# Mixer of a two-block transformer: projections in rounded parts, six buffers for high parts, one early expert place less

## The reference

```python
def split_cols(p): ...          # p = h @ w_in: q, f forward, f backward, v, gates
def gates(z, lb):               # f = lb + (1 - lb) * sigmoid(z); keys 1 - f, decays log(f)
def qv(p):                      # q = silu(p[2]) * 128 ** -0.5; v = p[5]
# each chunk: cum = cumsum(log f)
#   o = q * exp(cum) @ state + sum over earlier tokens of (q . k * exp(cum_t - cum_s)) v_s
#   state = exp(cum_end) * state + (k * exp(cum_end - cum)).T @ v
# out = rmsnorm(o) * silu(p[6]), merged with the attention under sigmoid(p[7]) and sigmoid(p[8])
```

## Time and profile before

| | us |
|---|---|
| median of 3 runs | 3784.51 |
| lowest, highest | 3781.16, 3787.37 |
| the profiled execution | 3779.92 |
| its span | 3778.1 |
| PE busy in the span | 3637.9 (96%) |
| DVE, ACT, POOL busy | 1917.7, 1146.6, 360.3 |

### The profile page before, as it was taken

One profiled execution on the slowest core, in us unless ns is written; L12 is line 12 of the kernel. 1 busy time (PEld: TensorE's weight loads), 2 busy tenths in 40 slices (PEclk: granted clock), 3 DMA queues, 4 the chain that ended last, 5 costly groups with the idle time before them and its releaser, 6 DMA issues.

```text
span 3778.1 us, 55586 instructions
## 1 busy us (share of the span) xinstructions
PE 3637.9 (96%) x23568; PEld 2589.5 (69%) x23568; DVE 1917.7 (51%) x3415; ACT 1146.6 (30%) x1733; POOL 360.3 (10%) x213
## 2 busy tenths in 40 slices
PE   8999999999999999999999999999899999999997
PEld 7799888888887998888987865767633333333333
DVE  4588576768664885767696333556421111111111
ACT  3243344444532433444445212333210000000011
POOL 0044300000000432000000000212000000000000
PEclk9899999999998999999999999999899999999999
DMA  5544344445446444444454312211489999999996
GB/s 200 211 174 163 135 168 177 160 177 181 169 153 227 164 163 139 158 178 178 175 172 171 133 66 100 90 67 64 163 371 421 427 428 427 427 428 427 428 427 271
DMA packets 81024, 846.24 MB, mean 224 GB/s; under 512 B 8896, under 2 KB 11072, under 8 KB 12512
## 3 DMA queue, kind: packets, MB, share of 16 engines
q1 hardware_dynamic: 80768, 842.60, 56.8%
HBM read 841.52 MB, written 1.05 MB: 223 GB/s over the span
## 4 chain that ended last, share of the span: by engine, by line
PE 83%; DMA 10%; DVE 4%; ACT 2%; issue 1%; POOL 0%; DVEq 0%; ACTq 0%; SPq 0%
PE bank L88 81%; DMA ring<-in_w_gu_dram 10%; ACT arena L114 1%; PE bank L101 1%; DVE arena L124 1%; DVE arena L138 1%; DVE arena L168 0%; DVE arena L156 0%; DVE arena L132 0%; DMA ring<-in_w_inA_dram 0%; ACT L114 0%; DVE arena L144 0%; DVE ring_rounded L124 0%; POOL ring_rounded L124 0%; DVE arena L130 0%
## 5 line engine op out<-in xcount | busy, mean ns | idle before, releaser
L88 PE MATMUL bank<-arena 128*128 128x32 f16 (+7 forms) x8020 | 922.2, 328 | 37.0 <-DVE arena L124 11.9
L88 PEld LDWEIGHTS bank<-arena 128*128 128x128 f16 (+4 forms) x8020 | 502.4, 132 | 451.3 <-issue 335.7
L124 DVE TENSOR_TENSOR arena<-arena 128x512 f16<-128x512 f16 (+6 forms) x768 | 531.9, 719 | 55.8 <-ACT arena L114 40.4
L114 ACT ACTIVATE arena<-bank 128x256 f32<-128x256 f32 (+2 forms) x443 | 203.0, 458 | 1164.3 <-PE bank L88 940.2
L88 PE MATMUL bank<-ring,arena 128*64 128x512 f32 (+1 forms) x1968 | 502.8, 596 | 39.7 <-DMA ring<-in_w_gu_dram 36.2
L88 PE MATMUL bank<-xhi,ring_rounded 128*128 128x256 f32 x1744 | 489.2, 280 | 0.0
L88 PE MATMUL bank<-xhi,uhi 128*128 128x256 f32 x1552 | 453.0, 292 | 6.5 <-DVE ring_rounded L124 5.8
L88 PE MATMUL bank<-xlo,uhi 128*128 128x256 f32 x1552 | 437.1, 282 | 0.0
L88 PEld LDWEIGHTS bank<-ring,arena 128*64 128x64 f32 (+1 forms) x1968 | 170.3, 144 | 361.2 <-issue 281.9
L88 PE MATMUL bank<-vhi,phi 128*128 128x512 f32 x1024 | 408.0, 398 | 2.0 <-DVE ring_rounded L124 2.0
L88 PE MATMUL bank<-vhi,plo 128*128 128x512 f32 x1024 | 403.5, 394 | 0.0
(11 more groups left out here) (144 smaller groups left out, 3216.9 us busy)
## 6 DMA issues: line engine op xcount, KB each, us to landing
ring<-in_w_gu_dram SPq DMA_DIRECT2D x97, 2048.0 KB, 23.8
ring<-in_peer_u_dram SPq DMA_DIRECT2D x128, 1024.0 KB, 6.7
ring<-in_peer_v_dram SPq DMA_DIRECT2D x128, 1024.0 KB, 5.1
arena<-in_w_dn_dram SPq DMA_DIRECT2D x62, 2048.0 KB, 22.4
arena<-in_w_gu_dram SPq DMA_DIRECT2D x43, 2048.0 KB, 22.3
ring<-in_w_hg_dram SPq DMA_DIRECT2D x14, 2048.0 KB, 8.4
ring<-in_w_mod_dram SPq DMA_DIRECT2D x12, 2048.0 KB, 7.8
ring<-in_w_inA_dram SPq DMA_DIRECT2D x8, 2048.0 KB, 7.8
```

Source lines behind the costliest of these rows:

```text
L88: i = self.e.matmul(o, l, r, start=start, stop=stop)
L114: self.e.activation(o, i, f, scale=scale, **kw).then_inc(self.sem, 1)
L124: self.e.tensor_tensor(o, a, b, op).then_inc(self.sem, 1)
```

## The change

Each projection of the state model becomes three rounded matmuls per slice. h is split into a high part (`uhi`, `xhi`) and a low part (`h_r`, on the place of h) after the gates of the attention are projected. Each task's weights, 1024 columns, are split into a high part, a copy to the rounded type on ACT (`act_high`), and a low part, weights minus high on POOL (`pool_low`), which takes the weights' own place. PE multiplies high by high, high by low, low by high. A v task becomes a quarter of the input slices for all tokens, and four v banks are copied out after the last.

The tasks are numbered 0 to 47 in PE's order (`in_turn`). There are six buffers for high parts, two in `xlo` and four in the ring place that the attention's last q weights leave; the ring is left with two places. `highs` sets how far the parts are made at each step: numbers 0 to 5 in the attention; 6 and 7 among the first f tasks; 8, 9 after the log, 10, 11 after the exp of the keys, 12, 13 before the kdT copies, 14 to 17 in the levels of unit 0. Unit 1: 18, 19 after the sigmoid, 20, 21 after the log, 22, 23 after the exp of the keys, 24, 25 before kdT, 26 to 29 in the levels. Unit 2: 30 to 32, 33 and 34, 35, 36 and 37, 38 to 41 likewise. Unit 3: 42, 43; 44, 45; none; 46, 47.

The tasks of unit 1's readout and of unit 2 change places: one q task in the readout, then three q and four v. The early expert piece is no longer fetched; the first two pieces come when all tasks are done ("hg parts").

```diff
+HIGHS = 6
@@
-        before_keys = {0: q_tasks(0) + v_tasks(0), 1: gate_tasks(0), 2: q_tasks(1) + v_tasks(1)[1:], 3: gate_tasks(1)[:6]}
+        before_keys = {0: q_tasks(0) + v_tasks(0), 1: gate_tasks(0), 2: q_tasks(1)[1:] + v_tasks(1), 3: gate_tasks(1)[:6]}
...
-        in_readout = {0: v_tasks(1)[0:1], 1: []}
+        in_readout = {0: q_tasks(1)[0:1], 1: []}
@@ pe_task
-            P.wait_ge(*at["landed", ("w_hg", kind, k)])
+            P.wait_ge(*at["hg split", kind, k, ct])
...
-                P.mm(b[:, 0:cols], [(w[:, dc, cs], hT[:, dc, 0:cols]) for dc in range(8)])
+                P.mm(b[:, 0:cols], [(w[:, dc, :], h) for dc in range(8) for w, h in
+                                    ((hi, h_high(dc)[:, 0:cols]), (hi, h_lo[:, dc, 0:cols]), (lo, h_high(dc)[:, 0:cols]))])
...
+        def act_high(i):
+            if i < len(in_turn):
+                kind, k, ct = in_turn[i]
+                A.wait_ge(*at["landed", ("w_hg", kind, k)])
+                if i >= HIGHS:
+                    A.wait_ge(*at["hg", *in_turn[i - HIGHS]])
+                A.act(task_high(kind, k, ct), task_of(kind, k, ct), ACT.Copy)
+                A.mark("hg high", kind, k, ct)
+        def pool_low(i):
...
+                G.wait_ge(*at["hg high", kind, k, ct])
+                G.tt(task_low(kind, k, ct), task_of(kind, k, ct), task_high(kind, k, ct).bitcast(F32), SUB, lag=FREE)
+                G.mark("hg split", kind, k, ct)
+        def highs(u, step, k=0):
+            a, n = number[before_keys[u][0]], len(before_keys[u])
+            till = {"first": min(a + 4, a + 3 + k), "sigmoid": a + 4, "log": a + 6, "keys": a + n, "before": a + n + 2,
+                    "level": a + n + (2, 3, 3, 4, 4, 5, 6)[k]}[step]
+            since = made[0]
+            made[0] = max(since, min(till, len(in_turn)))
+            return range(since, made[0])
@@ pool_mixer
+                for step in ("sigmoid", "log", "keys"):
+                    pool_lows(u, step)
...
+                pool_level(u, 0)
+                pool_level(u, 1)
+                pool_lows(u, "before")
                 for lv in range(7):
-                    pool_level(u, lv)
+                    if lv < 5:
+                        pool_level(u, lv + 2)
+                    pool_lows(u, "level", lv)
@@ sp_mixer
-            sp_moe_early()
+            ring.in_turn([ring.place["w_qb_r",] // 2, ring.place["w_hg", "f", 0] // 2])
```

More of the change, by code:

```diff
@@ L1902, in sp_mixer @@
                 sp_task(*task)
-            after_stage(S, "peer", 1)
-            sp_moe_early()
+            for p in (parts_at(), NSLOT):
+                ring.tenant[2 * p:2 * p + 2] = [("hg parts",)] * 2
+            ring.in_turn([ring.place["w_qb_r",] // 2, ring.place["w_hg", "f", 0] // 2])
+            sp_task(*before_keys[0][0])
             for name in "PVAG":
@@ L2226, in dve_mixer @@
             dve_rope(0)
+            for i in range(2):
+                dve_h_split(i)
             V.wait_ge(*at["q rope in"])
@@ L2395, in act_mixer @@
                     act_rms(x_rstd, 512, 256, "kv")
+            for i in range(2):
+                act_h_high(i)
             for h in range(8):
@@ L2410, in act_mixer @@
                 act_exp_p(i + 2)
+                if 4 <= i < 8:
+                    act_high(i - 4)
+            act_high(4)
+            act_high(5)
+            made[0] = 6
             end_stage_name(A, "A")
             after_attention(A)
-            for task in f_tasks(0):
+            for i, task in enumerate(f_tasks(0)):
                 act_task(*task)
+                act_highs(0, "first", i)
             for u, (hh, r) in enumerate(units):
@@ L2424, in act_mixer @@
                 A.mark("f log", u)
+                act_highs(u, "log")
                 A.wait_ge(*at["ends", u])
@@ L2430, in act_mixer @@
                 A.mark("kd exp", u)
+                act_highs(u, "keys")
                 if r == 0:
-                    for task in before_keys[u][:4]:
+                    for task in before_keys[u][:4 - hh]:
                         act_task(*task)
@@ L2437, in act_mixer @@
                     act_level(u, 1)
-                    for task in before_keys[u][4:]:
+                    for task in before_keys[u][4 - hh:]:
                         act_task(*task)
@@ L2444, in act_mixer @@
                     act_level(u, 1)
+                act_highs(u, "before")
                 for i in range(3):
@@ L2489, in pool_mixer @@
             end_stage_name(G, "G")
+            for i in range(6):
+                pool_low(i)
+            made[0] = 6
             after_attention(G)
+            for i in range(4):
+                pool_lows(0, "first", i)
             for u, (hh, r) in enumerate(units):
+                for step in ("sigmoid", "log", "keys"):
+                    pool_lows(u, step)
                 if u:
```

95 lines of the change are left out of this document (78 added, 17 removed).

## The result

| | before | after |
|---|---|---|
| median, us (range, runs) | 3782.8 (3780.0 to 3787.4, 4) | 3831.4 (3828.3 to 3833.3, 4) |
| ratio, 95% interval | | 1.0127 (1.0109 to 1.0144) |
| profiled execution, us; its span | 3779.9; 3778.1 | 3832.1; 3830.2 |
| mean granted clock of PE | 0.986 | 0.975 |
| PE busy, us | 3637.9 | 3620.2 |

The change makes the kernel **slower by 48.6 us**. The forecast was 3811.5, slower by 27 on a range up to 3830: right in sign, and the time lies 1.4 us above the range.

What follows compares the result with a forecast made beforehand. Experts were taken as HBM-bound behind the mixer; there PE bounds unit 0, PE and the key chain together later. Terms +0.5 - 4.5 + 2 + 12.4 + 8.5 + 8 gave +27 us, forecast 3811.5, range 3781 to 3830.

Steps and rivals of the forecast that it cites:

- What PE is spared: PE, 48 projection tasks: wide ones save 1.3 us, narrow ones 0.6, 45 us of PE work in all.
- Highs 0 to 5 fall between the exponentials: +0.5: Attention: highs fit the exponentials' idle times; their lows may hold DVE copies at the end, +0.5 us, bounds 0 and 2.
- Unit 0, -4.5: Unit 0 up to its levels: level 0's first product done at 73.6 us against 78.1, despite waits for parts.
- Unit 1, +12.4: Unit 1 up to its levels: later log, held scans, late lows 22 and 23, 49.6 us against 37.2.
- Unit 2, +8.5: Unit 2 up to its levels: some 15 us wait for low 30, held scans, 67.7 us against 59.2.
- Unit 3, +8: Unit 3 up to its levels: chain ends 6.5 us later, two highs before kdT counted as 1.5.
- Levels, +2: Levels of units 0 to 2: 5.2 saved, 4.5 waited, small ones; +0.7 us a unit carried, bounds -8 and +6.
- Place given up, 0: Ring place and early expert fetch given up: loads stay hidden, nothing lost; 5 us if not hidden.
- Scans held: Key chain: POOL's low parts lock out DVE's scans, eight taking near 10.6 us instead of 5.8 in units 0 to 2.
- Clock, "0, bounds 0 and +8": PE's granted clock: new standing lowers it, but mostly where the chain ends last; 0 us, bounds 0 and +8.
- Rival C: Whole kernel: full price with clock (+8) and the place not hidden (+5), +40 us, 3824; chance 9%.
- Rival A: Whole kernel: PE's work decides if parts are there when PE wants them, -21 us, 3763; chance 14%.

Runs made afterwards that it cites:

- ten, experiment 10: Experiment 3 plus the other high and low points moved to idle times, twelve lows on DVE, the others on POOL: 3783.4 us, ratio 1.0003.
- experiment 1: Changed kernel without the 48 low parts; the third product takes the high part again: 3781.3 us, ratio 0.9999.
- experiment 2: Changed kernel with all low parts made by DVE at the same points, none on POOL: 3834.5 us, ratio 1.0136.
- Experiment 3: Changed kernel with only the attention's parts moved: highs 0 to 3 around the last q projection's copies, lows 4 and 5 on DVE after the attention: 3827.2 us.
- experiment 9: Kernel before the change with only the ring place given up and no early expert piece, nothing in parts: 3781.4 us, ratio 1.0000.
- Experiment 6: Kernel before the change with two extra ACT copies ahead of the turned keys' copies in each of four units: 3795.6 us, ratio 1.0038.
- twelve: On top of ten, first two parts of the levels of units 0 and 2 made during v, lows 22 and 23 earlier: 3781.1 us, ratio 0.9998.
- 5: On top of Experiment 3, the two highs ahead of the turned keys' copies put behind them in all four units: 3811.9 us, ratio 1.0081.
- 4: Changed kernel with highs and lows 22, 23 moved to the log and 30, 31 into the first readout, lows on POOL: 3827.0 us, ratio 1.0112.

## Why the prediction was wrong in size

- **What PE is spared** was right as work: the four q tasks of unit 0 take 11.43 us in the trace of after (2325.24 to 2336.67), 2.86 each, as forecast. It was wrong as busy time: this fell by 17.7 us, not 45. Multiplied by the granted clock of its stretch, PE's busy time in the four units is 345 us before and 301 after, 44 less (an estimate from the two tables of stretches); as it stands it is 352 and 338. The rest went to the lower clock. Even ten shows 33 less, not 45.
- **"Highs 0 to 5 fall between the exponentials: +0.5"** is the first step that failed. The bound was taken from a copy. The scalings of DVE read one tile from SBUF, and the forecast took only instructions with two for lockable. They are held like the others, 2.5 for 0.49, and PE waits 2 to 4 us three times: the attention is 7.1 longer in the trace of after. Without lows (experiment 1) it is 1.9 longer, so 5.2 come with the lows; made by DVE at the same points (experiment 2) they cost as much. Experiment 3 gives back 3.7, and 3.6 by the medians.
- **Unit 0, -4.5**: -1.7. The 4.03 ahead of the states came as forecast (3.6). What it left out is the 1.6 that they take longer behind such a wait.
- **Unit 1, +12.4**: +16.3. Named rightly: highs ahead of the log, held scans (9.89; 10.6 forecast), the late lows 22 and 23, highs ahead of kdT. Missing: f held 4.0, with which the log ends at 12.6 us from the unit's start instead of 9.6; and the lower clock over the last two gate tasks and the states.
- **Unit 2, +8.5**: +14.6. The wait for low 30 was forecast with some 15 and is 12.8, the scans end at 43.7 for 42.9. So the front was nearly right in sum, though f is held 4.0 here too (6.28 for 2.29), where the forecast had 2.2 for three highs. Low 30 reaches PE at 27.7 us from the unit's start for 25.7, and PE ends v at 58.2 for 56. From there to the levels it needs 15.6 us where the sum had 11.7: waits of 0.8 and 5.1 ahead of the states for the 3.6 of the forecast, and 6.37 for the states, 1.7 more than at the full clock.
- **Unit 3, +8**: +12. The scans end at 23.8 us from the unit's start for 22.0, behind an f that is held, and the states take 1.6 more at the lower clock: 3.4 of the 4 that are missing. They were not run apart here.
- **Levels, +2**: +2.6, near in part by luck. The terms that were named, 5.2 saved and 4.5 waited, give a gain of 0.7 a unit; the +0.7 that was carried rests on "small ones" that were not added up. In each of these units the trace of after has one wait of 3.9 at level 4, behind which 16 matmuls take up to 3.2 us instead of 1.95, and none above 1 us at level 6.
- **Place given up, 0**: shown by experiment 9. **Scans held**: shown, 2.1 us for each low that meets them. The Trainium skill, "SBUF — State Buffer", section "Who interferes with whom", by which this was forecast, is borne out. The same section also says that `tensor_scalar` can lock with GpSimd when it runs in a two-port mode: the rows of f and of the attention agree that it locks, and a TENSOR_SCALAR of 128x2048 takes 1.23 us, as long as a subtraction of two tiles of 128x1024 (1.2), which fits such a mode. That half of the rule was not used.
- **Clock, "0, bounds 0 and +8"** is the term that was most mis-sized. The rows of the kernel before already had the pattern: stretches in which PE stood had 0.93 and 0.86. The mean clock fell from 0.986 to 0.975, and PE's busy time in ten against after prices it at about 15 us (an estimate, see experiment 10). Experiment 6 shows it without any parts: 9 us of added waits cost 13.6 (9.5 to 19).

Rival C (full price, clock and place, +40) came nearest, with the wrong second half: the place is free, the clock costs more. Rival A (PE's work decides, 3763) did not come in any kernel, but its condition was not fully met in any either: in ten PE no longer waits for low 30, but still 6.98 us for low 22, 4.10 in twelve. There units 1 and 3 take 4.8 and 2.3 more than before to their levels, and unit 0 takes 10 less. Of the signs that the forecast gave for itself, the scans (9.9 for 10.6), POOL's busy time in the four units (181 for 170) and the waits for low 22, low 30 and ahead of the states came.

## What to carry to other kernels

A part made "at a fixed point" costs its own time wherever that point lies in a chain that sets the end, and the order of two neighbours (copies ahead of the step that PE waits for, or behind it) was worth 14 us here. Price such a step with the clock that PE loses behind the longer wait, not by its length alone, and do not read the gain of moving something from the wait it ends: waits of 8.3 and 12.8 us were moved away for 3 us, which is within the uncertainty. Work that is given to GpSimd because it is idle is best laid where VectorE waits as well; ask first which VectorE instructions run beside it, those with one SBUF operand too.

## What the runs showed of the hardware

- A TENSOR_SCALAR of 128x512 with its one tile in SBUF takes 0.49 (0.57 with f's per-partition scalars) alone, and 2.4 to 2.6 when it meets a GpSimd subtraction of 128x1024, as long as that lasts.
- Eight TENSOR_TENSOR_SCANs of 128x256 (5.77) take 9.9 beside two such subtractions, 13.9 to 14.0 beside four. It works the other way as well: beside them POOL takes 2.66 a subtraction instead of 2.35 (10.64 for four).
- The 40 matmuls of 128x128 of the states took 4.70 behind a wait of 1.8 (unit 1 of before, unit 0 of 5; granted clock 1.00) and 6.33 behind one of 4.0 to 4.1 (units 0 and 1 of after, unit 1 of 6; clock 0.72 to 0.73, so at the half level, 1.2 of 2.4 GHz, for a part of them). Behind a wait as long they took 7.12 once, in 3, at 0.63. Behind a wait of 1.9 to 2.2 they took 6.33 in unit 3 of after and unit 2 of before, and 4.70 behind 1.8 in unit 3 of 4: what decides there is open.
